# The last expert's down projection in column quarters, its second half of weights in five loads, and y copied and combined in two steps

## What is computed

```python
def expert_step(acc, xs):
    wgu, bgu, wd, bd, g = xs
    hgu = tok @ wgu + bgu
    x_glu = jnp.minimum(hgu[:, 0::2], SWIGLU_LIMIT)
    x_lin = jnp.clip(hgu[:, 1::2], -SWIGLU_LIMIT, SWIGLU_LIMIT)
    act = x_glu * jax.nn.sigmoid(SWIGLU_ALPHA * x_glu) * (x_lin + 1.0)
    out = act @ wd + bd
    return acc + g[:, None] * out, None
...
h = rms_norm(h, g_final)
return h[:, N_META:]
```

## Time and profile before

| | before |
|---|---|
| median of three runs | 1020.49 us (1019.78 to 1022.28) |
| the profiled execution, its own time | 1020.46 us |
| its span in the trace | 1018.6 us |
| TensorE busy, share of the span | 984.6 us, 97% |
| share of the 16 DMA engines' span, main queue | 98.3% |
| mean granted TensorE clock | 0.998 |

### The profile page before, as it was taken

How to read it: one execution, slowest core, us unless ns; L and a number is a source line. 1 busy time by engine, 2 the same in 40 slices (tenths; PEclk the granted TensorE clock), 3 DMA queues, 4 the chain that set the end, 5 groups by cost and what they waited for, 6 DMA issues and landing times.

```text
span 1018.6 us, 11678 instructions
## 1 busy us (share of the span) xinstructions
PE 984.6 (97%) x4760; PEld 393.5 (39%) x4760; DVE 234.9 (23%) x618; ACT 162.8 (16%) x306; POOL 40.3 (4%) x81
## 2 busy tenths in 40 slices
PE   9999999999999999999999999999999999999996
PEld 8888533333333333333333333333333333323332
DVE  6976311111111111101112111111111111111122
ACT  5773311111110111001110100111111101100112
POOL 4830000000000000000000000000000000000000
PEclk9999999999999999999999999999999999999999
DMA  8999899999999999999999999999999999999996
GB/s 245 318 396 413 314 394 412 425 426 437 429 430 429 430 426 430 433 432 431 432 430 429 424 431 434 432 424 407 427 432 438 432 430 430 430 423 428 427 425 246
DMA packets 45593, 419.19 MB, mean 412 GB/s; under 512 B 6125, under 2 KB 22653, under 8 KB 25336
## 3 DMA queue, kind: packets, MB, share of 16 engines
q1 hardware_dynamic: 44824, 418.38, 98.3%
q10 hardware_dynamic: 736, 0.34, 0.1%
HBM read 417.66 MB, written 1.05 MB: 411 GB/s over the span
## 4 chain that ended last, share of the span: by engine, by line
PE 64%; DMA 29%; POOL 2%; ACT 1%; DVE 1%; SPq 1%; issue 1%; POOLq 0%; DVEq 0%; ACTq 0%
PE bank L1421 28%; DMA dn_ring<-in_w_down 21%; PE bank L1460 18%; DMA gu_ring<-in_w_gate_up 7%; PE bank L1395 4%; PE bank L1350 3%; PE bank L1255 3%; POOL reg L574 2%; PE bank L1236 2%; PE bank L1344 2%; ACT reg L743 1%; PE bank L1440 1%; PE bank L1434 1%; SPq L503 1%; SPq L504 0%
## 5 line engine op out<-in xcount | busy, mean ns | idle before, releaser
L1421 PE MATMUL bank<-gu_ring,reg 128*64 128x512 f32 x2048 | 451.1, 596 | 5.3 <-DMA gu_ring<-in_w_gate_up 5.3
L1421 PEld LDWEIGHTS bank<-gu_ring,reg 128*64 128x64 f32 x2048 | 143.5, 137 | 305.5 <-issue 293.6
L1460 PE MATMUL bank<-dn_ring,reg 128*64 128x512 f32 x760 | 170.6, 595 | 14.5 <-DMA dn_ring<-in_w_down 10.1
L1080 DVE TENSOR_SCALAR reg<-bank 128x256 f32<-128x256 f32 x64 | 24.2, 420 | 590.8 <-PE bank L1421 590.8
L1460 PEld LDWEIGHTS bank<-dn_ring,reg 128*64 128x64 f32 x760 | 52.9, 137 | 119.6 <-issue 97.0
L738 ACT ACTIVATE reg<-reg 128x512 f32<-128x512 f32 x30 | 18.9, 630 | 468.8 <-DVE reg L1080 468.8
L1395 PE MATMUL bank<-reg 64*128 64x512 f32 x256 | 63.9, 616 | 0.9 <-DVE reg L1142 0.9
L1460 PE MATMUL bank<-dn_odd,reg 128*64 128x512 f32 x256 | 58.6, 598 | 3.8 <-ACT reg L743 3.8
L1350 PE MATMUL bank<-xh,reg 128*64 128x512 f32 x248 | 58.5, 592 | 0.0
L745 ACT ACTIVATE reg<-bank 128x512 f32<-128x512 f32 x30 | 17.9, 597 | 227.5 <-PE bank L1460 227.5
L1236 PE MATMUL bank<-reg,gu_ring 128*128 128x272 f32 (+1 forms) x224 | 51.4, 389 | 0.0
(11 more groups left out here) (239 smaller groups left out, 472.2 us busy)
## 6 DMA issues: line engine op xcount, KB each, us to landing
gu_ring<-in_w_gate_up SPq DMA_DIRECT2D x46, 4096.0 KB, 30.0
dn_ring<-in_w_down SPq DMA_DIRECT2D x39, 2048.0 KB, 22.8
gu_ring<-in_w_gate_up SPq DMA_DIRECT2D x32, 2048.0 KB, 18.1
dn_odd<-in_w_down SPq DMA_DIRECT2D x15, 2048.0 KB, 29.3
dn_ring<-in_w_down SPq DMA_DIRECT2D x16, 1024.0 KB, 10.5
gu_ring<-in_w_in SPq DMA_DIRECT2D x16, 512.0 KB, 7.3
gu_ring<-in_w_gate_up SPq DMA_DIRECT2D x8, 1024.0 KB, 7.3
dn_ring<-in_w_out SPq DMA_DIRECT2D x4, 1024.0 KB, 8.5
```

Of the source, the lines that this page charges most:

```text
L1080: ins = V.tensor_scalar(half(xglu, b), glu_v[:, 0], 7.0, None, ALU.min)
L1421: ins = mm(gub[b][64 * h:64 * h + 64, :], xgT[:, j, :], gu_ring[:, s, j, 1024 * h + 512 * b:1024 * h + 512 * b + 512], start=False, stop=( ...
L1460: ins = mm(out[64 * h:64 * h + 64, :], a[:, at:at + SLOTS], w[:, 512 * h:512 * h + 512], start=(k == 0), stop=(k == KD - 1))
```

## The change

The loads of expert 31's second half become five: row 4, row 5, row 6, and row 7 in two pieces. A piece of row 7 holds, in each partition, columns 0 to 255 and 512 to 767 (or the 256 after each), so two runs of 1 KB where a row has one of 4 KB. The last expert's `down` has a function of its own, `last_down`: each row is multiplied in matmuls 256 columns wide, first quarter q = 0 of both column halves into bank `tb`, then q = 1 into bank `gub[0]`. Row 7's q = 1 waits for its own piece, and the last matmul of q = 0 raises `y0_ps`. VectorE copies q = 0 after `y0_ps` and q = 1 after `y_ps`. `final_combine` goes through token half 0 (q = 0, then q = 1) and then half 1, waits for the second copy only at its second step, and raises `bd_ps` once for each token half. TensorE's load of `n_x` moves from behind the last `down` to ahead of it; the branch stays behind. The diff, cut to what computes and waits:

```diff
@@ -508,10 +512,12 @@
             sp.dma_start(head_part(1, 1, 2), head_rows(NE - 1, 1, 2)).then_inc(row_in[2], 16)
             sp.dma_start(head_part(1, 2, 4), head_rows(NE - 1, 2, 4)).then_inc(head_in[1], 16)
             sp.wait_ge(dn_used, (NE - 2) * 2 + 2)
-            sp.dma_start(quarter_slot(0), quarter_rows(NE - 1, 0)).then_inc(tail_q[0], 16)
+            for j, landed in enumerate((tail_q[0], row5_in)):
+                sp.dma_start(dn_ring[:, 4 + j, :], dn_v[NE - 1, 1, :, D * j:D * (j + 1)]).then_inc(landed, 16)
             sp.wait_ge(y_ps, NE - 1)
-            for j in range(2):
-                sp.dma_start(dn_ring[:, 6 + j, :], dn_v[NE - 1, 1, :, D * (2 + j):D * (3 + j)]).then_inc(last_in[j], 16)
+            sp.dma_start(dn_ring[:, 6, :], dn_v[NE - 1, 1, :, 2 * D:3 * D]).then_inc(last_in[0], 16)
+            for q, landed in enumerate((last_in[1], fin_in)):
+                sp.dma_start(quarters_of(dn_ring[:, 7, :], q), quarters_of(dn_v[NE - 1, 1, :, 3 * D:4 * D], q)).then_inc(landed, 16)
 
             sp.wait_ge(q_ok, 1)
             n_x = sp.value_load(qi[0:1, XCOLS:XCOLS + 1], min_val=0, max_val=XCOLS - 1)
@@ -786,10 +792,10 @@
                 act.wait_ge(fin_sq, t + 1)
                 nc.scalar.activation(rstd3[:, t:t + 1], ssq3[:, t:t + 1], ACT.Sqrt, scale=1.0 / D, bias=eps_col).then_inc(rt3_ok, 1)
 
-            act.wait_ge(bd_ps, 2)
+            act.wait_ge(bd_ps, 1)
             square(0)
             root(0)
-            act.wait_ge(bd_ps, 4)
+            act.wait_ge(bd_ps, 2)
             act.wait_ge(fin_ev, 1)
             square(1)
             root(1)
@@ -1138,8 +1144,10 @@
                 two_experts(g)
             expert(NE - 2, 1, freed_after(NE // 2 - 1))
             expert(NE - 1, 0, freed_after(NE // 2 - 1), more=False)
+            v.wait_ge(y0_ps, 1)
+            V.tensor_copy(yv[:, 0:256], tb[:, 0:256]).then_inc(y_ok, 1)
             v.wait_ge(y_ps, NE)
-            V.tensor_copy(yv, tb[:, :]).then_inc(y_ok, 1)
+            V.tensor_copy(yv[:, 256:512], gub[0][:, 0:256]).then_inc(y_ok, 1)
             v.wait_ge(q_ok, 1)
             n_x = v.value_load(qi[0:1, XCOLS:XCOLS + 1], min_val=0, max_val=XCOLS - 1)
             with v.If(n_x > 0):
@@ -1164,7 +1172,7 @@
                 v.wait_ge(inv3_ok, t + 1)
                 V.scalar_tensor_tensor(outb[:, t, h], accb[t][b][:, :], rstd3[:, t:t + 1], gfin[:, h], ALU.mult, ALU.mult).then_inc(out_ok, 1)
 
-            v.wait_ge(bd_ps, 4)
+            v.wait_ge(bd_ps, 2)
             gained(1, 0)
             inverse(0)
             finished(0, 0)
@@ -1387,15 +1395,25 @@
                 first_gather(i).then_inc(first_ps, 1)
             c9 = slice(0, CAND)
 
-            def combine(n, last=False, tiles=range(TT)):
-
-                pe.wait_ge(y_ok, n + 1)
+            def final_combine():
+
+                for t in range(TT):
+                    for q in range(2):
+                        c = slice(256 * q, 256 * q + 256)
+                        if t == 0:
+                            pe.wait_ge(y_ok, NE + q)
+                        for h in range(2):
+                            ins = mm(accb[t][h][:, c], gT[64 * h:64 * h + 64, t * P:(t + 1) * P], yv[64 * h:64 * h + 64, c],
+                                     start=False, stop=True, skip_group_check=True)
+                    ins.then_inc(bd_ps, 1)
+
+            def combine(n, tiles=range(TT), copies=1):
+
+                pe.wait_ge(y_ok, n + copies)
                 for t in tiles:
                     for h in range(2):
                         ins = mm(accb[t][h][:, :], gT[64 * h:64 * h + 64, t * P:(t + 1) * P], yv[64 * h:64 * h + 64, :],
                                  start=False, stop=True, skip_group_check=True)
-                        if last:
-                            ins.then_inc(bd_ps, 1)
 
             def gate_up(n, s, loads, before, hooks=(), halves=False, freed=4, rows_out=False, rows_in=False):
 
...
+            def last_down():
+
+                pe.wait_ge(aT_ok, NE)
+                for k in range(KD):
+                    if k < 2:
+                        pe.wait_ge(row_in[1 + k], 32)
+                    elif k == 2:
+                        pe.wait_ge(head_in[1], NE // 2 * 16)
+                    elif k == 4:
+                        pe.wait_ge(tail_q[0], (FINE + 2) * 16)
+                    elif k == 5:
+                        pe.wait_ge(row5_in, 16)
+                    elif k == 6:
+                        pe.wait_ge(last_in[0], 16)
+                    w = (dn_odd if k < 4 else dn_ring)[:, k, :]
+                    at = (k % 4) * P + (k // 4) * SLOTS
+                    for q, y in enumerate((tb, gub[0])):
+                        if k == KD - 1:
+                            pe.wait_ge((last_in[1], fin_in)[q], 16)
+                        for h in range(2):
+                            ins = mm(y[64 * h:64 * h + 64, 0:256], last_actT[:, at:at + SLOTS], w[:, 512 * h + 256 * q:512 * h + 256 * q + 256],
+                                     start=(k == 0), stop=(k == KD - 1))
+                        if k == KD - 1 and q == 0:
+                            ins.then_inc(y0_ps, 1)
+                    if k in (3, 5):
+                        ins.then_inc(dn_used, 1)
+                    if k == 1:
+                        combine_30()
+                ins.then_inc(y_ps, 1)
+
...
@@ -1574,18 +1620,17 @@
             expert_up(NE - 2, 1, 4, NE - 3, hooks={5: combine_29}, tiles=(1,))
             gate_up(NE - 1, 0, 5, NE - 2)
             down(NE - 2, 0, NE // 2, FINE + 1, quarters=True, split={0: row_in[0], 2: head_in[0]}, hooks={5: turn_31})
-            down(NE - 1, 1, NE // 2, FINE + 2, quarters=True, last=True,
-                 split={0: row_in[1], 1: row_in[2], 2: head_in[1]}, hooks={1: combine_30}, a=last_actT, out=tb)
             n_x = pe.value_load(qi[0:1, XCOLS:XCOLS + 1], min_val=0, max_val=XCOLS - 1)
+            last_down()
             with pe.If(n_x > 0):
                 gather(NE, 2 * NE + 1)
                 turn_gathered(NE)
                 with pe.Fori(0, n_x) as q:
-                    expert_up(q + NE, 0, q + (NE // 2 - 4), q + (NE - 1), halves=True)
+                    expert_up(q + NE, 0, q + (NE // 2 - 4), q + (NE - 1), copies=2, halves=True)
                     down(q + NE, 0, q + (NE // 2 + 1), q + (NE - 2 - FINE + 1))
-                    pe.wait_ge(y_ok, q + (NE + 1))
+                    pe.wait_ge(y_ok, q + (NE + 2))
             pe.wait_ge(gT_ok, NE)
-            combine(NE - 1, last=True)
+            final_combine()
 
 
 def kernel(**inputs):
```

More of the change, by code:

```diff
@@ L261, in build @@
         row_in, row_used = [sem(f"row_in{j}") for j in range(GP)], sem("row_used")
[L262 removed]
+        last_in, row5_in = [sem("last_in0"), sem("last_in1")], sem("row5_in")
         dn_used = sem("dn_used")
@@ L288, in build @@
         gT_ps, gT_ok, aT_ps, aT_ok = sem("gT_ps"), sem("gT_ok"), sem("aT_ps"), sem("aT_ok")
-        y_ps, y_ok = sem("y_ps"), sem("y_ok")
-        tail_in, gfin_in, fin_dve, fin_sq, fin_ev, bd_ps, ms3_ok, rt3_ok, inv3_ok, out_ok, out_act, out_done = (
-            sem(n) for n in ("tail_in", "gfin_in", "fin_dve", "fin_sq", "fin_ev", "bd_ps", "ms3_ok", "rt3_ok", "inv3_ok",
+        y_ps, y_ok, y0_ps = sem("y_ps"), sem("y_ok"), sem("y0_ps")
+        tail_in, gfin_in, fin_in, fin_sq, fin_ev, bd_ps, ms3_ok, rt3_ok, inv3_ok, out_ok, out_act, out_done = (
+            sem(n) for n in ("tail_in", "gfin_in", "fin_in", "fin_sq", "fin_ev", "bd_ps", "ms3_ok", "rt3_ok", "inv3_ok",
                              "out_ok", "out_act", "out_done"))
@@ L1441, in act_turned, with down @@
                 ins.then_inc(aT_ps, 1)
-            def down(n, odd, heads, tails, quarters=False, last=False, moved=False, split=None, hooks=(), a=actT, out=db):
+            def down(n, odd, heads, tails, quarters=False, moved=False, split=None, hooks=()):
                 pe.wait_ge(aT_ok, n + 1)
@@ L1450, in down @@
                         pe.wait_ge(head_in[odd], heads * 16)
-                    if last and k >= 6:
-                        pe.wait_ge(last_in[k - 6], 16)
-                    elif quarters and k in (4, 6):
+                    if quarters and k in (4, 6):
                         pe.wait_ge(tail_q[k // 2 - 2], (2 if k == 4 and n == 0 else tails) * 16)
@@ L1459, in down @@
                     for h in range(2):
-                        ins = mm(out[64 * h:64 * h + 64, :], a[:, at:at + SLOTS], w[:, 512 * h:512 * h + 512],
+                        ins = mm(db[64 * h:64 * h + 64, :], actT[:, at:at + SLOTS], w[:, 512 * h:512 * h + 512],
                                  start=(k == 0), stop=(k == KD - 1))
@@ L1466, in down, with expert_up @@
                 ins.then_inc(y_ps, 1)
-            def expert_up(n, s, loads, before, hooks=(), before_turn=None, before_down=None, tiles=range(TT), **pieces):
+            def last_down():
[26 more added lines that the diff above has]
+                ins.then_inc(y_ps, 1)
```

(3 more changed lines are left out.)

2 lines of the change are left out of this document (added).

## The result

The changed kernel takes 1022.42 us (median of 14 runs, 1020.08 to 1025.16); the kernel before, run beside it, 1020.20. The ratio is 1.0021, 95% interval 1.0014 to 1.0029: some 2.1 us slower, between 1.4 and 3.0. The prediction was 1019.7, in a range of 1018.8 to 1021.2, with the main case 0.75 faster. The time lies above the range, and on the other side of the kernel before than the forecast. It is within the 0.3% that the chances counted as no change, but the interval excludes 1.

What follows compares the result with a forecast made beforehand. TensorE was taken to bound the kernel, with DMA right behind. Terms -0.81 + 0.03 + 0 + 0 = -0.78, or -0.75 with half the possible DMA loss, took 1020.46 to 1019.7 us, range 1018.8 to 1021.2.

Steps and rivals of the forecast that it cites:

- main case: Whole kernel: the shorter tail behind the last down saves 0.75 us, giving 1019.7 us; chance 0.74.
- Meanwhile TensorE combines q = 0 of token half 0, two pairs, from about E + 0.15: After E, the last down matmul's end: combine overlaps the second copy, `gained` at E + 2.19 instead of 3.00, saving 0.81.
- a pair costs 0.216 us: Last combine: price of two 256-column matmuls in half-arrays, from 16 full-array records of 256 lasting 3.62 us.
- The first rival: TensorE before the last down: the moved register load stalls it, +1.07 us, ending at 1020.8; chance 0.12.
- the second rival: Behind the last down: the two copies do not overlap with the combine, saving only 0.3, 1020.2 us; chance 0.09.
- The twice 32 records of the last down: Last down: 64 records of 256 instead of 32 of 512 cost +0.03 us, bounds 0 to +0.25.
- Row 7 was there: Last down's weights: row 7 in two pieces of 1 KB runs arrives in time, likeliest loss 0, at most 0.1 us.
- the third rival: Row 7's loads: small pieces pay a fixed time one after another, +2.3 us, ending at 1022.0; chance 0.05.
- half of the possible DMA loss: Row 7's weight loads: half of the at most 0.1 us, allowed for in going from -0.78 to -0.75.
- `gained` starts 2.2 us behind: Sign of being right: in the changed profile VectorE's `gained` starts 2.2 us after the last down matmul.
- The last mark: Sign of failure: the whole run moves by more than a microsecond before 995 us, where nothing was changed.

Runs made afterwards that it cites:

- fall_through: Changed kernel with the last combine written twice, first on the path that runs straight on, nothing left out: 1020.08 us, ratio 1.0006.
- old_fall_through: Kernel before the change with its own last combine written twice, first on the path that runs straight on: 1019.53 us, ratio 1.0001.
- new_again: The changed kernel once more, unaltered, for a second look at the clock: 1023.48 us, one run.
- skip_near: Changed kernel with the never-run code for extra items cut from TensorE's `If`: 1019.53 us against 1019.69, ratio 0.9999.
- new_moved_192: Changed kernel with 192 already-satisfied waiting instructions added on TensorE, measured twice: 1019.08 us, ratio 0.9992, and 1019.82 us, ratio 0.9999.
- straight_moved_80: Changed kernel with the last combine also on the straight path and 80 waiting instructions added: 1019.48 us, ratio 0.9996.

## Why the prediction was wrong

**The step that failed** is in the part on what follows the last down: "Meanwhile TensorE combines q = 0 of token half 0, two pairs, from about E + 0.15". It let the combine start as soon as its copy was there. Between the last down and the combine stands the branch, which the sum put at nothing: its 0.36 us in the earlier trace rows were over at 1009.25, under the last matmuls. (Of the 0.14 in the chain, which I took for a wake-up, 0.04 is left in fall_through and old_fall_through, where the combine stands on the straight path.) I carried that price over although the change put 64 more instructions ahead of it. The branch became 3.66 us, and the combine started at E + 2.74, where it starts at E + 0.19 with a fast branch (+2.55). The same step counted "a pair costs 0.216 us"; at the lower clock eight pairs took 3.61 instead of 2.00, +1.6. With the 0.1 below these are the 4.27 us between 6.46 and 2.19. In the timed runs the loss was smaller, 2.1 us against the kernel before, than the 3.46 and 3.41 us of the two profiles (the changed kernel and new_again). With the slow branch and the upper clock it would be 1.9 (the combine 0.19 + 2.00 us long becomes 2.74 + 2.00, so `gained` is at E + 4.86 instead of 3.00), so part of the runs may have had that clock; which ones, the runs don't tell.

None of the three rivals was this one, and the instruction stream stands in none of them. That the third's 1022.0 is nearest to the measured 1022.42 is luck, as its mechanism did not occur. The first rival put a stall on the register load; here it started within 0.02 us of the wait for row 6 of expert 30 (999.27 and 999.29), took 0.49 us, and the next down followed without a gap, as the main case said.

**The other steps held.** With a fast branch `gained` starts at E + 2.30 (skip_near, new_moved_192: 1011.17 - 1008.87) or, straight on, E + 2.22, for 2.19 forecast and 3.00 before. The 0.1 lies in the combine: it starts 0.19 after E, for 0.15, and its eight pairs run without a gap in 2.00 us, for the 1.93 from 0.15 to 2.08 in the forecast, so TensorE and not the second copy sets the end. The price of a pair, 0.216, came from the full array, while the kernel before had shown 1.99 us for this very work. The copies took 0.42 us each, back to back (the second rival is out). The twice 32 records of the last down cost 5.39 to 5.40 us for 5.37 (+0.03 forecast). Row 7 was there: the last weight packet of the changed kernel ended at 1008.98, and no wait shows in the 3.62 us; its 1 KB packets took 46 ns in the median beside 159 ns for 4 KB, and the third rival is out. The change proper is thus worth 0.7 us in the profile (3.00 - 2.30, less some 0.02 for the longer down; 0.78 forecast). The timed runs with a fast branch and nothing left out, 0.9992 and 0.9999 (new_moved_192) and 0.9996 (straight_moved_80), lie between 0.1 and 0.8 us of gain, but none excludes 1, so no version here is shown to beat the kernel before. The sum itself has a small slip: -0.78 with half of the possible DMA loss of 0.1 is -0.73 and not -0.75, which changes nothing above.

Of the marks named in advance the first ("`gained` starts 2.2 us behind") failed and found the fault. The copies, rows 2 to 7 and the register load came as named there. The last mark, a run that moves by more than a microsecond before 995 us, was met too: expert 30's rows 0 to 3 began at 992.78 instead of 991.57. In new_again they began at 991.18, with the same loss behind E, so it has no part in the fault. Such a mark should have been put on the branch itself.

## What to carry to other kernels

Code that is longer can cost time where a taken branch follows: ask of each branch on the critical path how many instructions lie between it and its target, and whether an edit ahead of it moves it across a block's edge. A fast branch in the profile before says nothing about one at another place. Put the common path where it runs straight on, and look also at where the fetch then falls: among the last stores it cost more in the profile than the change had saved. And when a late stretch is judged, count from the last event that both versions share, since the end of the last down lay at places 3.7 us apart in the profiles here.

## What the runs showed of the hardware

- A taken branch on TensorE over some 300 instructions (an estimate, from the matmuls of the skipped code and their weight loads) took 0.35, 0.95 or 3.4 to 3.9 us, by its position alone; one not taken 0.08, one to a target just behind it 0.21.
- Each branch that waited ended 1.41 to 1.43 us after the end of a 16 KB packet of instructions, in six profiles.
- The lower clock came in the combine after 2.6 to 3.6 us of idle in three profiles of four, and nearly doubled its time (3.6 to 3.8 us for 2.0).
- A fetch of 16 KB of instructions, 1.06 us long, among the output stores went with a last wait of 3.8 us instead of 2.3 to 2.4, in one profile.
- With the unused code left out of TensorE's program the time outside the span was 1.8 to 3.5 us in eleven runs instead of 1.8 to 2.0; unexplained.
